# Up projections of six feed-forwards: both parts of x in one 512-column product

## The reference

```
def conv_ffn(h, w_up, conv_w, conv_b, w_down):      # first block, layers 0 and 1
    u = h @ w_up                                     # 1024 -> 2 * 2816
    c = conv_b + u_pad[:, 0:n] * conv_w[0] + ...     # three taps over the tokens
    gate, val = jnp.split(c, 2, axis=-1)
    return (jax.nn.silu(gate) * val) @ w_down
...
    g, u = jnp.split(h @ w_gu, 2, axis=-1)           # second block, two in each layer
    return (jax.nn.silu(g) * u) @ w_down
```

## Time and profile before

| | us |
|---|---|
| median of 3 runs | 2358.9 (2356.7 to 2364.66) |
| span of the profiled execution | 2356.1 |
| PE busy | 2238.9 (95%) |
| VectorE busy | 1505.8 (64%) |
| ScalarE busy | 1111.5 (47%) |
| chain that ended last, share of PE | 83% |

### The profile page before, as it was taken

One profiled execution on the slowest core, in us unless ns is written; L12 is line 12 of the kernel. 1 busy time (PEld: TensorE's weight loads), 2 busy tenths in 40 slices (PEclk: granted clock), 3 DMA queues, 4 the chain that ended last, 5 costly groups with the idle time before them and its releaser, 6 DMA issues.

```text
span 2356.1 us, 40460 instructions
## 1 busy us (share of the span) xinstructions
PE 2238.9 (95%) x17488; PEld 2137.2 (91%) x17488; DVE 1505.8 (64%) x2188; ACT 1111.5 (47%) x1341; POOL 339.3 (14%) x292
## 2 busy tenths in 40 slices
PE   8988999998789999999999999999999999998998
PEld 7877899997679999999998789999999998898998
DVE  5665687833458788566766657566666556656665
ACT  5445544535455445334646455335334455555333
POOL 2760000045000000000535210000000015310000
PEclk9989999998899999999999999999999999999999
DMA  8642355543224555555653444555555643353552
GB/s 267 195 157 90 118 182 185 179 145 108 72 90 167 193 179 186 172 192 176 163 167 114 129 163 147 175 188 170 179 197 179 168 148 117 117 185 129 182 193 90
DMA packets 314660, 374.21 MB, mean 159 GB/s; under 512 B 23127, under 2 KB 280931, under 8 KB 313331
## 3 DMA queue, kind: packets, MB, share of 16 engines
q1 hardware_dynamic: 309555, 354.88, 46.2%
q0 software_dynamic: 3424, 11.50, 1.7%
q10 hardware_dynamic: 1504, 5.26, 0.6%
HBM read 362.43 MB, written 9.18 MB: 158 GB/s over the span
## 4 chain that ended last, share of the span: by engine, by line
PE 83%; DVE 9%; ACT 5%; issue 2%; DMA 0%; ACTq 0%; SPq 0%; DVEq 0%
PE banks L868 23%; PE banks L869 22%; PE banks L871 22%; PE banks L901 3%; PE banks L902 3%; DVE wlo L1766 3%; PE banks L905 2%; ACT whi L1338 2%; PE banks L1116 2%; PE banks L1154 1%; PE banks L1140 1%; PE banks L1036 1%; DVE wk L2301 1%; PE banks L1023 1%; PE banks L878 1%
## 5 line engine op out<-in xcount | busy, mean ns | idle before, releaser
L868 PE MATMUL banks<-x_hi,wlo 128*128 128x256 f32 (+1 forms) x4344 | 1104.3, 287 | 22.5 <-DVE wlo L1766 6.9
L869 PE MATMUL banks<-x_lo,whi 128*128 128x256 f32 (+1 forms) x4344 | 1094.8, 285 | 0.0
L1338 ACT ACTIVATE whi<-raw 128x2048 fp32r<-128x2048 f32 (+1 forms) x340 | 637.7, 1878 | 618.0 <-PE banks L871 570.3
L868 PEld LDWEIGHTS banks<-x_hi,wlo 128*128 128x128 f32 (+1 forms) x4344 | 840.4, 193 | 42.6 <-issue 19.6
L869 PEld LDWEIGHTS banks<-x_lo,whi 128*128 128x128 f32 (+1 forms) x4344 | 841.1, 194 | 0.0
L1766 DVE TENSOR_TENSOR wlo<-raw,whi 128x2048 fp32r<-128x2048 f32 (+2 forms) x292 | 656.9, 2260 | 167.5 <-ACT whi L1338 167.4
L871 PE MATMUL banks<-x_hi,whi 128*128 128x256 f32 x4344 | 688.8, 284 | 0.0
L871 PEld LDWEIGHTS banks<-x_hi,whi 128*128 128x128 f32 x4344 | 596.9, 193 | 3.2
L836 POOL TENSOR_TENSOR wlo<-raw,whi 128x512 fp32r<-128x512 f32 x184 | 238.2, 1332 | 1168.0 <-ACT whi L1338 1168.0
L901 PE MATMUL banks<-x_hi,wlo 128*128 128x256 f32 (+1 forms) x632 | 169.6, 302 | 23.2 <-DVE xT L1795 7.4
L902 PE MATMUL banks<-x_lo,whi 128*128 128x256 f32 (+1 forms) x632 | 162.6, 291 | 0.0
(11 more groups left out here) (252 smaller groups left out, 1977.7 us busy)
## 6 DMA issues: line engine op xcount, KB each, us to landing
raw<-in_ffn_w_gu SPq DMA_DIRECT2D x88, 1024.0 KB, 5.1
raw<-in_ffn_w_down SPq DMA_DIRECT2D x66, 1024.0 KB, 5.2
raw<-in_ffn_w_up SPq DMA_DIRECT2D x44, 1024.0 KB, 5.1
raw<-in_w_in SPq DMA_DIRECT2D x42, 1024.0 KB, 5.3
raw<-in_ca_w_kv SPq DMA_DIRECT2D x16, 1024.0 KB, 5.2
raw<-in_od_w_in SPq DMA_DIRECT2D x12, 1024.0 KB, 5.1
raw<-in_ev_w_in SPq DMA_DIRECT2D x10, 1024.0 KB, 9.1
raw<-in_w_in SPq DMA_DIRECT2D x20, 512.0 KB, 5.1
```

The lines of the kernel that those rows point to most:

```text
L868: eng.matmul(out, a[1], b[0], start=first and i == 0, stop=False, skip_group_check=True)
L869: eng.matmul(out, a[0], b[1], start=False, stop=False, skip_group_check=True)
L1338: eng.activation(whi[s % SETS][:, 0:ch["n"]], raw[i % SLOTS][:, 0:ch["n"]], ACT.Copy).then_inc(S["weights_hi"], 1)
```

## The change

x's two parts become one tile of 2 x 8 x 256, so that x_hi and x_lo of one k can be read as one operand of 512 columns. In the up projections of all six feed-forwards each k then takes two matmuls in place of three: whi times both parts (512 columns, a whole bank) and wlo times x_hi (256 columns, added to the bank's first half). The second half of the bank holds whi\*x_lo, which has to be added to the first.

- An output tile of 256 tokens now fills a bank. The two gate tiles of a step take both gate banks and the two val tiles both val banks, so up(j) waits for step j - 1 to be taken out, not j - 2.
- ScalarE copies the second halves of two banks to SBUF (`rest`, new, twice a step); VectorE adds them to the first halves, waits for that, and multiplies by the norm's scale in place. Before, one VectorE instruction did all.
- up(0) is written anew (`up_first`): for each pair of k it makes gate tile a, the two val tiles, gate tile b. The gate is complete last, the val just before it.
- The norm's sum goes to bank 3 in these stages, and up(1) no longer waits for `norm_ready` itself.
- The down projections and all other stages are as before.

```
+            def both_parts(bank, operands, k0, end):
+                for k in range(k0, end):
+                    w, x = operands[k]
+                    eng.matmul(bank, w[0], x, start=k == 0, stop=False, skip_group_check=True)
+                    m = eng.matmul(bank[:, 0:SEQ], w[1], x[:, 0, :], start=False, stop=k == len(operands) - 1, skip_group_check=True)
+                return m
...
+                def up_first():
+                    a, b = st["first_tile"], 1 - st["first_tile"]
+                    for p in range(KT // 2):
+                        eng.wait_ge(S["xs_ready"], KT * n + 2 * p + 2)
+                        for part, i, bank in (("gate", a, gate_banks[:, a, :]), ("val", 0, val_banks[:, 0, :]), ("val", 1, val_banks[:, 1, :]),
+                                              ("gate", b, gate_banks[:, b, :])):
+                            if p == 0:
+                                arrived(steps[0][part][0])
+                                if part == "gate":
+                                    free = last[0 if i == a else 1]
+                                    eng.wait_ge(S[free["taker"]], free["taken"])
+                            if p == KT // 2 - 1 and part == "val" and i == 0:
+                                sum_squares(st["norm"])
+                            m = both_parts(bank, tile(0, part, i), 2 * p, 2 * p + 2)
+                            if p == KT // 2 - 1 and part == "val" and i == 1:
+                                m.then_inc(S["ffn_up"], 1)
+                    m.then_inc(S["ffn_gate"], 1)
...
                 def up(j):
-                    if j >= 2:
-                        eng.wait_ge(S["gate_scaled"], s0 + j - 1)
-                        eng.wait_ge(S["val_scaled"], s0 + j - 1)
-                    if j == 1:
-                        eng.wait_ge(S["norm_ready"], st["norm"]["n"] + 1)
...
-                    for part, bank, signal in (("gate", gate[j % 2], "ffn_gate"), ("val", post_bank[j % 2], "ffn_up")):
+                    for part, tiles, signal, free in (("gate", gate_banks, "ffn_gate", "gate_scaled"), ("val", val_banks, "ffn_up", "val_scaled")):
                         arrived(steps[j][part][0])
-                        for o, operands in mms(j, part):
-                            m = product(bank[:, o], operands, True, True)
+                        eng.wait_ge(S[free], s0 + j)
+                        for i in range(2):
+                            m = both_parts(tiles[:, i, :], tile(j, part, i), 0, KT)
                         m.then_inc(S[signal], 1)
...
+            def rest(half, made, tiles, s, used, done):
+                eng.wait_ge(S[made], s + 1)
+                if s:
+                    eng.wait_ge(S[used], s)
+                eng.activation(wk[:, 6 + half, :].rearrange("p (n c) -> p n c", c=SEQ), tiles[:, :, SEQ:], ACT.Copy).then_inc(S[done], 1)
...
+                    split_upto(st["steps"][j]["gate"][0] + 2)
+                    rest(0, "ffn_gate", gate_banks, s, "gate_scaled", "gate_rest")
                     split_upto(st["steps"][j]["val"][0] + 2)
+                    rest(1, "ffn_up", val_banks, s, "val_scaled", "val_rest")
...
-                    def scaled(half, bank):
-                        return eng.tensor_tensor(wk[:, half, :].rearrange("p (n c) -> p n c", c=SEQ), bank[:, :].rearrange("p (n c) -> p n c", c=SEQ),
-                                                 norms, ALU.mult)
+                    def scaled(half, tiles):
+                        u, more = (wk[:, i, :].rearrange("p (n c) -> p n c", c=SEQ) for i in (half, 6 + half))
+                        eng.wait_ge(S[("gate_rest", "val_rest")[half]], s + 1)
+                        step(eng.tensor_tensor(u, tiles[:, :, 0:SEQ], more, ALU.add))
+                        hold()
+                        return eng.tensor_tensor(u, u, norms, ALU.mult)
```

More of the change, by code:

```diff
@@ L177, in build @@
         xT = sb("xT", [P, KT, SEQ])
-        X = [(sb(f"x{n}_hi", [P, KT, SEQ], F32R), sb(f"x{n}_lo", [P, KT, SEQ], F32R)) for n in range(2)]
+        xparts = [sb(f"x_parts{n}", [P, 2, KT, SEQ], F32R) for n in range(2)]
+        X = [(x[:, 0], x[:, 1]) for x in xparts]
         ft = sb("ft", [P, 23, SEQ])
@@ L220, in build @@
         lin_bank, post_bank = banks[4:6], banks[6:8]
+        gate_banks, val_banks, ffn_total = bank_pairs[2], bank_pairs[3], banks[3]
         na_skew = nc.dram_tensor("na_skew", [56, 64, P], F32)
@@ L597, in ffn @@
                 then["pairs"] = [("x_added", o0 + p + 1) for p in range(4)]
+            norm["total"] = ffn_total[:, 0:SEQ]
             stage("ffn", join=True, steps=steps, s0=s0, d0=d0, o0=o0, scale=scale, conv=conv_layer, norm=norm, then=then, act=act,
-                  gate=[lin_bank[(n_of["lin"] + j) % 2] for j in range(2)], last=[units_of[n_of["lin"] - 2 + j] for j in range(2)],
+                  first_tile=n_of["lin"] % 2, last=[units_of[n_of["lin"] - 2 + j] for j in range(2)],
                   c0=number("conv", FF_STEPS) if conv_layer is not None else 0)
@@ L1233, in ffn, with tile @@
             def ffn(st):
-                steps, s0, gate = st["steps"], st["s0"], st["gate"]
-                def mms(j, part):
+                steps, s0 = st["steps"], st["s0"]
+                x, last, n = xparts[st["norm"]["buf"]], st["last"], st["norm"]["n"]
+                def tile(j, part, i):
                     w = steps[j][part][1]
-                    return [(slice(i * SEQ, (i + 1) * SEQ), [([v[:, k, i * P:(i + 1) * P] for v in w], [x[:, k, :] for x in X[st["norm"]["buf"]]])
-                                                            for k in range(KT)]) for i in range(2)]
@@ L1241, in up @@
[L1241 to L1247 removed]
+                    return [([v[:, k, i * P:(i + 1) * P] for v in w], x[:, :, k, :]) for k in range(KT)]
+                def up_first():
[15 more added lines that the diff above has]
+                    m.then_inc(S["ffn_gate"], 1)
@@ L1248, in up @@
+                def up(j):
                     if j == 0:
-                        pairs = [(gate[0], mms(0, "gate"), steps[0]["gate"][0], lambda: eng.wait_ge(S[st["last"][0]["taker"]], st["last"][0]["taken"])),
-                                 (post_bank[0], mms(0, "val"), steps[0]["val"][0], lambda: None)]
-                        for m, signal in zip(as_it_comes(pairs, "xs_ready", KT * st["norm"]["n"], 2, st["norm"]), ("ffn_gate", "ffn_up")):
-                            m.then_inc(S[signal], 1)
+                        up_first()
@@ L2277, in ffn @@
                     s = st["s0"] + j
-                    gate, val = st["gate"][j % 2], post_bank[j % 2]
                     split_upto(st["steps"][j]["gate"][0] + 2)
```

15 lines of the change are left out of this document (7 added, 8 removed).

## The result

| | before | after |
|---|---|---|
| median of 4 runs, us | 2360.5 (2356.7 to 2364.7) | 2380.6 (2378.9 to 2387.0) |
| ratio, 95% interval | | 1.0088 (1.0069 to 1.0107) |
| span of the profiled execution, us | 2356.1 | 2385.1 |
| mean granted clock in it | 0.973 | 0.966 |

The changed kernel takes 20.1 us more. The prediction was slower, by 14.9 us, at 2374 us; its sign holds, and 2380.6 us lies in its range of 2354 to 2385. (It counted from the median of three runs of before, 2358.9 us; a fourth run moved that to 2360.5.) The profiled execution of the changed kernel is the slowest of its four (the other spans are 2377.1 to 2379.9 us), so its 29.0 us over the span of before are not all due to the change.

What follows compares the result with a forecast made beforehand. PE bounds the 17.28 us steady steps, with 1.44 us of room in VectorE's convolution loop. A -8.4, B +9.2 and C +14.1 give +14.9 on 2356.1: 2371.0, plus 2.8 for the median: 2373.8 us; range 2354 to 2385.

Steps and rivals of the forecast that it cites:

- A: Up projections' matmuls: a group takes 0.354 us instead of 0.360; -8.4 us in the four plain feed-forwards.
- B: Start of each feed-forward: PE waits 2.3 us ahead of gate(1) for gate(0) to leave its banks; +9.2 in plain ones.
- the norm would be no rival: Feed-forward start: the norm's scale would be ready at 918.4, so it would not come last ahead of the scale on gate.
- C: Two convolution feed-forwards: two additions a step make VectorE's loop 17.28 us and the bound; +7.8 and +6.3, together +14.1 us.
- the second loses one such step less: Second convolution feed-forward reaches its steady step a step earlier, so loses about 1.5 us less than the first: +6.3 us.
- The last chain's 13.65 us: First convolution feed-forward's last step, to the end of the activation's parts: 13.65 + 1.44 = 15.09 us, 15.15 before.
- Rival 1: Up-projection matmuls: the weight load sets the 0.120 us, so a group takes 0.327; 2335.8 us in all; chance 12%.
- Rival 4: Convolution loop is not the bound: additions or copies cost less or fall into VectorE's 2.15 us wait; 2360.1 us; chance 6%.
- Rival 3: Up-projection matmuls give next to nothing: 0.240 or 0.2375 us for 512 columns; 2382.2 or 2378.7 us; chance 15%.
- Rival 2: Up-projection matmuls: a fixed 0.013 us for each matmul, so a group takes 0.347; 2363.9 us; chance 17%.

Runs made afterwards that it cites:

- Experiment 1: Chains of fp32r matmuls alone, the whole computation left out: 0.120 us for 256 columns, 0.227 for 512, 0.354 for a pair in turn.
- experiment 3: Changed kernel with gate tiles ahead of val tiles in up(0)'s last pair of k, and the norm's sum ahead of all four: 2367.3 us, ratio 1.0018.
- experiment 7: Changed kernel without VectorE's two additions a step, the second halves still computed and copied but left out of the result: 2359.2 us, ratio 0.9987.
- experiment 6: Kernel before with the change in the four plain feed-forwards alone, the convolution ones as before: 2367.5 us, ratio 1.0026.

## Why the prediction was right, step by step

- **A** (0.354 us a group, 2.1 us less in each feed-forward): measured 0.353, 2.3 us less. The sum's term is right, its ground is not. It was read from the ends of matmuls, which a profile models, while their starts are measured. Experiment 1 shows a fixed 13 ns and a slope of 2.4 GHz from 256 columns on, and 7 ns that come from the alternation. With the true costs of chains alone I would have had 0.347 and 2363.9, too low by 17 us. That 0.354 came out was luck: a second effect, which no row of before could show, made up for the wrong one.
- **B** (a gap of 2.3 us, released by the scale on gate): 2.33 us, released by L2320. The path was right to the link: copy, addition, scale. That the norm would be no rival held too, though by 0.2 us only (the addition waits 0.19 us for the copy), and experiment 3 shows it as next in line.
- **C** (VectorE's loop 15.84 + 1.44 = 17.28, PE 17.09): 17.30 and 17.07; without the additions 15.84 (experiment 7). At the addition on gate the first convolution feed-forward lost 0.70 us by step 0 (predicted 0.7), then 1.82 (2.04), 1.46 (1.44), 1.45 (1.44), 2.73 (1.44) and 1.34 (1.3), the second one 0.70, 1.83, 1.46, 1.46 and 1.31. That the second loses one such step less was forecast, but its reason is the half clock at 758.8 in the trace of before, which had lengthened that feed-forward by 1.5 us. The last chain's 13.65 us should by its own terms have been 15.15 - 1.35 = 13.80, which makes 15.24 of the 15.09; measured were 15.18.
- **What was missing.** C's term was 14.1 us and measured 19.2, B's and A's in the plain ones 0.8 and measured 3.1. Nearly all of that is half clock in the profiled execution, of which the prediction says nothing. The step that lost 2.73 follows the stretch from 319.9 to 326.7: PE came late with val and VectorE waited 1.18 us for the copy. From the last addition to the end I had 0.6 us less than before, and both lost 1.3: the parts of the activation are made 15.18 us behind the addition (predicted 15.09), but the last down projection, which had to wait for them (PE idle 2.58 us) as forecast, then runs its first 3.4 us at 1.2 GHz, at 463.0 and 917.2, some 1.7 us each. With 1.3 + 2 x 1.7 + 2 x 1.5 = 7.7 us for the clock the sum of 14.9 becomes 22.6, the 22.3 that the six feed-forwards of the profiled execution lost. The other three executions, 5 to 8 us shorter, have no trace, so how much half clock is in the median's 20.1 us is not shown.

Rival 1 (the weight load) falls by experiment 1: at 256 columns no load sets the pace, though at 224 and below something does, at 0.111. Rival 4 falls by the 17.30 us loop. Rival 3's time, 2379 to 2382, is nearest to the result, but not by its mechanism: the groups did give 6.6 ns. Rival 2's fixed cost is true of a chain of one size, but its time is not, because of the alternation.

## What to carry to other kernels

Before a faster matmul form is built, look at which engine has how much room in each loop: here 1.44 us of room in VectorE's loop was just what the form's two extra additions took, so the steady steps gained nothing and the early ones lost; and the same form in the loops with 6 us of room, with its banks freed early, gained 0.4 to 0.5%. A double use of banks makes a producer wait for the step right behind it; order the first step so that what is waited for is complete first. And price every gap that an edit opens in TensorE's work twice: once for its length, and once for the chance that the clock falls behind it.

## What the runs showed of the hardware that I had not expected

- Gaps of 1.9 to 3.9 us in PE's work were followed in some cases by 3.4 us at 1.2 GHz, once by 6.8 (behind 3 of the 6 starts here and 3 of the 4 in experiment 6; behind none of the 6 in experiment 3, with gaps of about 1.5 us). What tells the cases apart is open: the gaps of the four plain starts are alike to 0.01 us, and so are the two of 1.87 us in the trace of before. That a shorter gap makes half clock rarer is not shown by so few cases.
- fp32r matmuls in chains: 0.111 us at 128, 192 and 224 columns, then 0.013 + columns / 2.4 GHz from 256 to 512. In turn with 256-column ones, a 512-column matmul takes 0.236 in place of 0.227 and its partner 0.117 in place of 0.120; blocks of eight take 4 of the 6 ns a pair away.
- A GpSimd subtraction of 128x512 pieces (1.56 us each) adds up to 0.98 us to each VectorE instruction on SBUF operands beside it, and none to one that reads PSUM.
